# Sample-state product of the state-space phase in two f32r passes, with own room for the last group's states and tail rows

## The chip, the cores and the metric

The kernel runs on one core of a Trainium2 chip. The metric is the device time of one execution in microseconds; lower is better. The engines go by their short names: PE (TensorE, with PEld for its weight loads), DVE (VectorE), ACT (ScalarE), POOL (GpSimd), SP (SyncE, which issues most transfers; ACT issues the others).

## The reference, cut to what matters

Two layers run over a prompt of 1024 positions and 8 sample sequences of 8 positions each: a retention layer and a state-space (SSD) layer. The change is in the second. Per head, with keys `bm`, queries `cm`, values `v` and the log decay `log_a`:

```python
log_a = dt * (-jnp.exp(a_log))
v = xs * dt[..., None]
y, s_new = chunked_linear_recurrence(cm, bm, v, log_a, s0)
# inside it, per chunk (for the samples one chunk of 8 positions per sequence):
s_new = jnp.exp(cum[:, -1, :])[..., None, None] * s + jnp.einsum('bjhd,bjh,bjhe->bhde', kc, tail, vc)
```

For each of the 8 sequences the new sample state is the old one, decayed, plus keys times decayed values. The sum over the positions is the sample-state product. The outputs are y, the new states and the last three rows ahead of the convolution ("tail rows", `conv_prompt` and `conv_sample`, 27 rows of 4096 channels).

## The kernel before

The program runs in phases on one core: the first projection, the retention, its output projection (tag p2), then `phase_ssd`, then the last output projection (tag p4, `phase_mix`). Every engine has its own list of instructions, written out by hand and run in order; semaphores tie them together. `held` and `wait_ge` are waits at the head of an engine's list, so everything behind them on that engine stands too.

`phase_ssd` goes through 8 groups of 4 heads, each with 128 state rows and 4 x 64 = 256 value columns, and in each group through 8 steps c = 0 to 7, one per chunk of 128 prompt positions. In step c the samples' sequence c is done as well, so that sequences and chunks share the steps. While group g is worked on, PE also does the input projection of group g + 1 in 24 units, three per step, each of 24 f32r matmuls (`unit`, L1578); the last group (7) has none, and loads the weights of the output projection instead (`weights.load` on SP, 16 loads of 512 KB; `weights.high` on ACT and `weights.low` on DVE split them).

The samples of a group have their own chain, in step 0. PE turns keys and values (`turn`), ACT copies them to `btoks` (64 positions x 128) and `xtoks` (`by_tokens`), POOL makes the decayed values `vts` (`decayed_values`), DVE makes the sample mask, ACT its exponentials (`decay`), and DVE the decayed scores (`decay_scores`). For sequence c, ACT's `own` (L1878) multiplies the keys with a 0/1 column of that sequence into `bm`, and PE's `sample` (L1612 and L1615) makes four products of 8 columns with the old state `s_in` and then the sample-state product of `bm` (stationary) and `vts` (moving, 256 columns) in f32, over 128 rows of which the lower 64 are zero. DVE's `sample_state` adds the decayed old state (POOL's `s_mid`), and ACT stores the result. `sample(g, 0)` stands in step 1, ahead of that step's first unit; the other sequences c stand at the end of step c.

The states are loaded by SP into two slots (`load_state`, L1464); in each step the load for c + 2 waits until the slot is used, and in group 7 it stands behind three weight loads. In group 7 PE also turns 512 columns of the tail rows per step into PSUM (L1679), ACT copies them to `tail_rows` (27 x 512, L1885) and stores them with two transfers (`conv_rows_out`); the next copy waits for the stores before, and PE's next turn for the copy. At the end of the phase ACT waits for its stores. Behind step 7 DVE scales the first tile of the output projection (`next_tile.scale_all`, L2566), when ACT has made its roots (`next_tile.roots`), and the output projection begins with L2731.

Of the kernel before, what the change touches and what calls it, by code (L numbers as in the profile page):

```python
# [5 lines left out]
F32 = mybir.dt.float32  # L6
# [4 lines left out]
P = 128  # L11
# [1274 lines left out]
def phase_ssd(nc, sb, ps, sem, A, O, block0, xn_dram, params, rows_dram, dtail, lnb, etot, etot_s, g_dram, ss_dram, weights, next_tile, stale):  # L1286
# [11 lines left out]
    with ExitStack() as ctx:  # L1298
        SL = 4
        DH = 2  # L1300
        hi, lo, raw, whi, wlo, mid, th = block0.shared
        zb = block0.zb
        sb(ctx, "room_zb1", [P, NT6, CINW], F32)
        tails = sb(ctx, "p3tails", [P, CT, CTAIL], F32)
        tail_rows = sb(ctx, "p3tail_rows", [CTAIL, BANK], F32)

# [4 lines left out]
        seqcol = sb(ctx, "s_seqcol", [NS, DB], F32)  # L1311
# [20 lines left out]
        bm = sb(ctx, "s_bm", [P, 2, P], F32)  # L1332
        vt, vts = sb(ctx, "s_vt", [P, 2, SHG, SHD], F32), sb(ctx, "s_vts", [P, SHG, SHD], F32)
# [26 lines left out]
                 "sb_add", "b_own",  # L1360
# [6 lines left out]
        early, consts, passed, zeroed = sem("s_early"), sem("s_consts"), sem("s_passed"), sem("s_zeroed")  # L1367
        tails_turned, tails_taken, tails_stored = sem("s_tails_turned"), sem("s_tails_taken"), sem("s_tails_stored")
# [58 lines left out]
        def freed(eng, G):  # L1427

            if not isinstance(G, int) or G >= 2:
                held(eng, q["gated"], 9 * (G - 1) + B, passed)  # L1430

# [4 lines left out]
        with nc.Block() as block:  # L1436
            @block.sync
            def _(sp):
# [38 lines left out]
                def group(g, first=False, more=True, beyond=True):  # L1477
                    for c in range(NCH):
# [27 lines left out]
                        if c + 2 < NCH or more:  # L1506
                            load_state(g + (c + 2) // NCH, (c + 2) % NCH, 8 * g + c + 1)
# [22 lines left out]
                for dst, name in ((least_s, "least_s"), (seqcol, "seqcol")):  # L1530
                    sp.dma_start(dst[:], A[name]).then_inc(consts, 16)
# [30 lines left out]
            def _(pe):  # L1562
# [40 lines left out]
                def sample(g, c, par):  # L1603

                    s = c % 2
                    held(pe, q[f"sin{s}"], 16 * (4 * g + c // 2 + 1) + B, passed)
# [4 lines left out]
                    for k in range(NX):  # L1611
                        nc.tensor.matmul(xs_ps[:, k, c * OWN:(c + 1) * OWN], s_in[:, s, 2 * k:2 * k + 2, :].rearrange(  # L1612
                            "p h n -> p (h n)"), zb[par][:, 1, own], start=True, stop=True)
# [10 lines left out]
                def group(g, par, first=False, more=True):  # L1624
                    for c in range(NCH):
# [8 lines left out]
                        if c == 1:  # L1634
                            held(pe, q["vt"], prep(g, NCH) + 1 + B, passed)
                            sample(g, 0, par)
                        if more:
                            unit(g + 1, 3 * c)

# [30 lines left out]
                        else:  # L1670
                            sample(g, c, par)
                        if not more:
# [3 lines left out]
                            if c:  # L1676
                                pe.wait_ge(tails_taken, c)
                            for k in range(BLK):
                                last = nc.tensor.transpose(pr_ps[0:CTAIL, 0, k * P:(k + 1) * P], tails[:, c * BLK + k, :],  # L1679
# [69 lines left out]
                pe.wait_ge(zeroed, 8)  # L1749
# [11 lines left out]
            def _(act):  # L1761
# [58 lines left out]
                def by_tokens(g, c):  # L1820
# [10 lines left out]
                    nc.scalar.activation(b_dst[0:r, :], t_ps[0:r, 0:P], ACT.Copy).then_inc(q["tok"], 1)  # L1831
# [43 lines left out]
                def own(g, c):  # L1875

                    act.wait_ge(q["sb_mm"], 8 * g + c - 1 + B)
                    nc.scalar.activation(bm[0:NS, c % 2, :], btoks[:, :], ACT.Copy,  # L1878
                                         scale=seqcol[:, c:c + 1]).then_inc(q["b_own"], 1)

                def conv_rows_out(c):
                    act.wait_ge(tails_turned, c + 1)
                    if c:
                        dma_wait(act, tails_stored, 2 * c)
                    nc.scalar.activation(tail_rows[:, :], pr_ps[0:CTAIL, 0, :], ACT.Copy).then_inc(tails_taken, 1)  # L1885
                    act.wait_ge(tails_taken, c + 1)
                    at = slice(c * BANK, (c + 1) * BANK)
                    act.dma_start(O["conv_prompt"][0, 0, :, at], tail_rows[0:TAP - 1, :]).then_inc(tails_stored, 16)
                    act.dma_start(O["conv_sample"][0, :, :, at].rearrange("b w c -> (b w) c"),
                                  tail_rows[TAP - 1:CTAIL, :]).then_inc(tails_stored, 16)  # L1890

                def group(g, par, first=False, more=True, beyond=True):
                    for c in range(NCH):
# [125 lines left out]
                act.wait_ge(zeroed, 8)  # L2019
# [17 lines left out]
                dma_wait(act, tails_stored, 2 * NCH)  # L2037

            @block.gpsimd
            def _(pool):  # L2040
# [53 lines left out]
                def group(g, par, first=False, more=True):  # L2094
                    for c in range(NCH):
# [21 lines left out]
                        held(pool, q[f"sin{c % 2}"], 16 * (4 * g + c // 2 + 1) + B, passed)  # L2117
                        held(pool, q["sb_add"], 8 * g + c + B, passed)
                        nc.gpsimd.tensor_tensor(s_mid[:, :, :], s_in[:, c % 2, :, :],
# [20 lines left out]
                nc.gpsimd.memset(bm[NS:P, :, :], 0.0).then_inc(zeroed, 1)  # L2140
                nc.gpsimd.memset(vts[NS:P, :, :], 0.0).then_inc(zeroed, 1)
# [860 lines left out]
```

## Time and profile before

| | us |
|---|---|
| median of 3 runs (lowest, highest) | 2138.38 (2137.99, 2140.6) |
| profiled execution, its own time | 2143.32 |
| its span | 2141.5 |
| PE busy / DVE / ACT / POOL | 2042.8 / 1299.1 / 891.1 / 386.8 |
| mean granted PE clock | 0.976 |

The groups 0 to 6 of `phase_ssd` lie between about 1172 and 1873 us of the span, group 7 between 1873 and 1941, and the last output projection behind that. A row of a timeline has its start in us from the start of the span, its length, the engine, the line, the operation, output and inputs by name, their shapes and a count; in brackets stands the idle time ahead of it with what ended it. An f32 matmul shows as two instructions. The length of a matmul includes time in the pipeline, so the time that one holds PE is read from start to start. The profiled execution is one execution, slower than the median of the runs by 4.9.

### The profile page before, as it was taken

The numbers are of one execution on the slowest core, as the hardware profiler recorded it, in microseconds if no ns is written. First come the engines' busy times: TensorE is split into PE (matmuls) and PEld (weight loads), VectorE is DVE, ScalarE is ACT, GpSimd is POOL, SyncE is SP. The second block draws the span as 40 slices with busy tenths as digits, with TensorE's granted clock in tenths as the row PEclk, the third lists the DMA queues.
The fourth block names the chain that finished last, engine by engine and source line by source line (L and its number), as shares of the span: only waits on it lengthen the run. The fifth ranks groups of instructions, "written<-read, shape, count | busy, mean of one in ns | idle before, by whom it ended". The sixth has DMA issues, their size and how long they took to land. (4 is left out here: it accounts for less than half of the span.)

```text
span 2141.5 us, 40784 instructions
## 1 busy us (share of the span) xinstructions
PE 2042.8 (95%) x14070; PEld 1887.9 (88%) x14070; DVE 1299.1 (61%) x1929; ACT 891.1 (42%) x1947; POOL 386.8 (18%) x558
## 2 busy tenths in 40 slices
PE   6999999999899998999889999999999999978998
PEld 6999999999778776788789999999999999966887
DVE  7755899776456567233244757685767676675422
ACT  6221212333344355233344555554555555466331
POOL 0200000000122221000001434342434333350000
PEclk9999999999999998999999999999999999988999
DMA  4433333332688798243622333333333333284341
GB/s 134 132 103 103 91 101 108 107 112 82 206 278 275 248 314 296 88 143 110 176 49 62 93 85 85 84 87 85 94 93 80 96 80 88 69 263 137 115 126 40
DMA packets 387153, 274.10 MB, mean 128 GB/s; under 512 B 117714, under 2 KB 342706, under 8 KB 386922
## 3 DMA queue, kind: packets, MB, share of 16 engines
q1 hardware_dynamic: 338806, 242.77, 38.4%
q10 hardware_dynamic: 48144, 28.76, 4.4%
q8 instruction: 112, 1.84, 0.4%
q14 instruction: 91, 0.74, 0.1%
HBM read 184.59 MB, written 86.88 MB: 127 GB/s over the span
## 5 line engine op out<-in xcount | busy, mean ns | idle before, releaser
L1578 PE MATMUL p3acc_ps<-xn2hi,p3whi 128*128 128x272 f32 x1536 | 461.2, 300 | 6.2 <-ACT p3mid L1780 3.7
L1578 PE MATMUL p3acc_ps<-xn2lo,p3whi 128*128 128x272 f32 x1536 | 445.5, 290 | 0.0
L1578 PE MATMUL p3acc_ps<-xn2hi,p3wlo 128*128 128x272 f32 x1536 | 445.4, 290 | 0.0
L269 PE MATMUL p1ps<-x1hi,w1hi 128*128 128x272 f32 x1288 | 373.3, 290 | 4.7 <-issue 3.1
L269 PE MATMUL p1ps<-x1hi,w1lo 128*128 128x272 f32 x1288 | 373.1, 290 | 0.0
L269 PE MATMUL p1ps<-x1lo,w1hi 128*128 128x272 f32 x1288 | 372.1, 289 | 0.0
L1578 PEld LDWEIGHTS p3acc_ps<-xn2hi,p3whi 128*128 128x128 f32 x1536 | 292.3, 190 | 7.6 <-issue 7.2
L1578 PEld LDWEIGHTS p3acc_ps<-xn2lo,p3whi 128*128 128x128 f32 x1536 | 292.6, 191 | 0.2
L1578 PEld LDWEIGHTS p3acc_ps<-xn2hi,p3wlo 128*128 128x128 f32 x1536 | 291.8, 190 | 0.0
L269 PEld LDWEIGHTS p1ps<-x1hi,w1hi 128*128 128x128 f32 x1288 | 243.6, 189 | 5.1 <-issue 5.1
L269 PEld LDWEIGHTS p1ps<-x1hi,w1lo 128*128 128x128 f32 x1288 | 244.0, 189 | 0.0
L269 PEld LDWEIGHTS p1ps<-x1lo,w1hi 128*128 128x128 f32 x1288 | 243.6, 189 | 0.0
L2174 DVE SCALAR_TENSOR_TENSOR p3zb<-p3mid,params,p3zb 128x1112 f32<-128x1112 f32 x96 | 139.1, 1449 | 32.3 <-ACT p3zb L1792 18.8
L2064 POOL TENSOR_TENSOR s_gn<-s_yd,p3zb 128x256 f32<-128x256 f32 (+1 forms) x72 | 66.7, 926 | 316.0 <-DVE s_yd L2247 296.3
L419 ACT ACTIVATE y1sums<-p1ps 128x544 f32<-128x544 f32 x23 | 14.4, 625 | 262.2 <-PE p1ps L269 256.0
L1780 ACT ACTIVATE p3mid<-p3acc_ps 128x272 f32<-128x272 f32 x96 | 38.1, 397 | 135.6 <-PE p3acc_ps L1578 135.3
L1184 POOL MEMSET r_vlo<- 64x512 f32 x1 | 0.5, 519 | 480.9 <-POOLq L195 480.9
L2870 DVE TENSOR_TENSOR p4h<-p4h,p4acc 128x1024 f32<-128x1024 f32 (+1 forms) x9 | 11.0, 1220 | 119.1 <-PE p4acc L2731 104.3
L2731 PE MATMUL p2acc<-w2hi,p2ghi 128*128 128x512 f32 x256 | 80.7, 397 | 2.5 <-DVE p2glo L2845 2.5
L2731 PE MATMUL p4acc<-w4hi,p4ghi 128*128 128x512 f32 x256 | 80.0, 394 | 2.8 <-DVE p4glo L2845 2.8
L2731 PE MATMUL p2acc<-w2lo,p2ghi 128*128 128x512 f32 x256 | 79.8, 394 | 0.0
L2731 PE MATMUL p2acc<-w2hi,p2glo 128*128 128x512 f32 x256 | 79.5, 392 | 0.0
(330 smaller groups left out, 4367.4 us busy)
## 6 DMA issues: line engine op xcount, KB each, us to landing
w1raw<-in_ret_w_in SPq DMA_DIRECT2D x48, 512.0 KB, 5.0
p3raw<-in_ssm_w_in SPq DMA_DIRECT2D x48, 512.0 KB, 4.4
ret_vg<-y1out SPq DMA_DIRECT2D x32, 512.0 KB, 3.2
r_vg<-ret_vg SPq DMA_DIRECT2D x32, 512.0 KB, 5.0
r_sin<-in_state_ret SPq DMA_DIRECT2D x32, 512.0 KB, 6.1
out_ret_sample<-r_sout ACTq DMA_DIRECT2D x32, 512.0 KB, 6.5
s_cr<-sums SPq DMA_DIRECT2D x64, 256.0 KB, 3.4
ret_qk<-y1out SPq DMA_DIRECT2D x16, 512.0 KB, 3.7
```

The costliest lines, as they stand in the source:

```text
L269: last = nc.tensor.matmul(bank[:, 2 * at + i, 0:HB], w[s][:, idx, k, :], x[:, idx, k, i * HB:(i + 1) * HB], start=(k == 0 and j == 0), sto ...
L419: nc.scalar.activation(s1, slot(0), ACT.Copy).then_inc(s1_done, 1)
L1184: nc.gpsimd.memset(vlo[NS:P, :].bitcast(F32), 0.0).then_inc(zeroed, 1)
L1578: last = nc.tensor.matmul(pr_ps[:, n % 2, 0:TB], wt[:, j % 2, k, :], x[:, k, b * TB:(b + 1) * TB], start=(k == 0 and i == 0), stop=(k == K ...
L1780: last = nc.scalar.activation(mid[:, j % 2, TAP - 1 + b * TB:TAP - 1 + (b + 1) * TB], src, ACT.Copy)
L2064: nc.gpsimd.tensor_tensor(gn[:, slot(c), :, 0:width(c)], yd[:, :, 0:width(c)], zb[par][:, ZS:NT6, cols(c)], ALU.mult).then_inc(q["gated"], 1)
L2174: nc.vector.scalar_tensor_tensor(zb[par][:, j, 0:PW], mid[:, j % 2, w:w + PW], params[:, bass.ds(channel(G, j), 1), w], zb[par][:, j, 0:PW ...
L2731: last = nc.tensor.matmul(acc[0:r, t % 2, cols], x[:, t % 2, k, 0:r], wt[:, k, cols], start=(k == 0 and j == 0), stop=(k == KI - 1 and j = ...
L2870: nc.vector.tensor_tensor(h[0:r, t % 2, :], h[0:r, t % 2, :], acc[0:r, t % 2, :], ALU.add).then_inc(added, 1)
```

## The change

In `sample` the f32 product becomes two f32r products into the same sums. Keys and values are split into a high half, rounded to f32r, and the rest. The first product has the high key half on rows 0 to 63 and the low one on rows 64 to 127 (masked together by `own`, over 128 rows), against the high value half on both; the second has the high keys against the low values, over 64 rows. Once per group ACT copies the keys again as `bhl` (in `by_tokens`), DVE subtracts the low keys (`sample_keys_low`, behind `outputs(g, 0)` and ahead of the sample mask), ACT copies the values twice into `vhi` (`sample_values_high`, ahead of the sample exponentials) and DVE subtracts the low values (`sample_values_low`, behind `project` of step 0). `own(g, 0)` moves behind ACT's `project` of step 0, and waits for the low keys. `sample(g, 0)` moves behind the first unit of step 1 and waits for the low values (`v_low`).

In group 7 the states 2 to 7 go to a room of their own, and SP issues their six loads in step 0 ahead of the gain and the weights, once the projection is done. The tail rows get a room of 27 x 4096 and two PSUM banks by turns; they leave in two stores at the end of step 7. The room lies where the split weights go later. Two clears on POOL drop out, as no row of `bm` and `vts` is padding any more.

```diff
@@ sync
+        if c == 0:
+            sp.wait_ge(q["p_mm"], NU * SG + B)
+            for x in range(2, NCH):
+                sp.dma_start(s_in_last[:, x - 2, :, :], A["state_ssm"][0, x, g * SHG:(g + 1) * SHG, :, :
+                                   ].rearrange("h n p -> n h p")).then_inc(last_in, 16)
             sp.wait_ge(q["fin"], NT6 * SG + B)
...
-                        if c + 2 < NCH or more:
+                        if more:
                             load_state(g + (c + 2) // NCH, (c + 2) % NCH, 8 * g + c + 1)
@@ tensor, sample
-                    nc.tensor.matmul(sb_ps[:, 0:W], bm[:, s, :], vts[:, :, :].rearrange("p h n -> p (h n)"),
-                                     start=True, stop=True).then_inc(q["sb_mm"], 1)
+                    nc.tensor.matmul(sb_ps[:, 0:W], bm[:, s, :], vhi[:, :, :].rearrange("p h n -> p (h n)"), start=True, stop=False)
+                    nc.tensor.matmul(sb_ps[:, 0:W], bm[0:NS, s, :], vlo[:, :, :].rearrange("p h n -> p (h n)"),
+                                     start=False, stop=True).then_inc(q["sb_mm"], 1)
@@ tensor, group
-                        if c == 1:
-                            held(pe, q["vt"], prep(g, NCH) + 1 + B, passed)
-                            sample(g, 0, par)
                         if more:
                             unit(g + 1, 3 * c)
+                        if c == 1:
+                            held(pe, q["v_low"], g + 1 + B, passed)
+                            sample(g, 0, par, more)
...
-                            if c:
-                                pe.wait_ge(tails_taken, c)
+                            if c >= 2:
+                                pe.wait_ge(tails_taken, c - 1)
@@ scalar, by_tokens
+                    if c == NCH:
+                        last = nc.scalar.activation(bhl[0:NS, :], t_ps[0:NS, 0:P], ACT.Copy)
+                    last.then_inc(q["tok"], 1)
@@ scalar, own and the new copies
-                    nc.scalar.activation(bm[0:NS, c % 2, :], btoks[:, :], ACT.Copy,
+                    nc.scalar.activation(bm[:, c % 2, :], bhl[:, :], ACT.Copy,
                                          scale=seqcol[:, c:c + 1]).then_inc(q["b_own"], 1)
+                def sample_values_high(g):
+                    held(act, q["vt"], prep(g, NCH) + 1 + B, passed)
+                    nc.scalar.activation(vhi[0:NS, :, :], vts[:, :, :], ACT.Copy)
+                    nc.scalar.activation(vhi[NS:P, :, :], vts[:, :, :], ACT.Copy).then_inc(q["v_high"], 1)
@@ scalar, conv_rows_out
-                    if c:
-                        dma_wait(act, tails_stored, 2 * c)
-                    nc.scalar.activation(tail_rows[:, :], pr_ps[0:CTAIL, 0, :], ACT.Copy).then_inc(tails_taken, 1)
...
+                    nc.scalar.activation(tail_rows[:, c * BANK:(c + 1) * BANK], pr_ps[0:CTAIL, c % 2, :], ACT.Copy).then_inc(tails_taken, 1)
+                    if c == NCH - 1:
+                        act.wait_ge(tails_taken, NCH)
+                        act.dma_start(O["conv_prompt"][0, 0, :, :], tail_rows[0:TAP - 1, :]).then_inc(tails_stored, 16)
+                        act.dma_start(O["conv_sample"][0, :, :, :].rearrange("b w c -> (b w) c"),
+                                      tail_rows[TAP - 1:CTAIL, :]).then_inc(tails_stored, 16)
@@ scalar, group
                         if c == 0:
                             by_tokens(g, NCH)
-                            act.wait_ge(q["tok"], prep(g, NCH) + 1 + B)
-                            own(g, 0)
                         if more:
                             project(g + 1, 3 * c + 2, 1 - par, beyond)
+                        if c == 0:
+                            held(act, q["b_low"], g + 1 + B, passed)
+                            own(g, 0)
                         square(g, c)
                         if c == 0:
+                            sample_values_high(g)
                             decay(g, NCH, decs)
@@ vector
+                def sample_keys_low(g):
+                    held(dve, q["tok"], prep(g, NCH) + 1 + B, passed)
+                    held(dve, q["b_own"], 8 * g + B, passed)
+                    nc.vector.tensor_tensor(bhl[NS:P, :], btoks[:, :], bhl[0:NS, :], ALU.subtract).then_inc(q["b_low"], 1)
+                def sample_values_low(g):
+                    held(dve, q["v_high"], g + 1 + B, passed)
+                    nc.vector.tensor_tensor(vlo[:, :, :], vts[:, :, :], vhi[0:NS, :, :], ALU.subtract).then_inc(q["v_low"], 1)
...
                         outputs(g, c, par)
                         if c == 0:
+                            sample_keys_low(g)
                             held(dve, q["ins"], 16 * (g + 1) + B, passed)
                             dve.wait_ge(q["y_mm"], 9 * g + B)
                             mask(g, NCH, crws, decs, least_s[:, :])
                             decay_scores(g, NCH, decs)
                         if c + 1 < NCH and more:
                             project(g + 1, 3 * c + 2, 1 - par, beyond)
+                        if c == 0:
+                            sample_values_low(g)
```

## Rows read from the trace of the kernel before

**Rows 1.** Busy time by stages; the first line names the columns
```profile
core 0: us, PE busy (x) PEld busy (x) DVE busy (x) ACT busy (x) POOL busy (x), PEclk, DMA share, GB/s
...
1575.00:1677.00 102.00, 102.00 (x813) 100.68 (x812) 69.92 (x115) 53.65 (x135) 39.26 (x55) 1.00 0.34 87
...
1873.00:1941.00 68.00, 44.95 (x257) 37.78 (x255) 47.94 (x99) 42.28 (x112) 29.94 (x44) 0.80 0.74 226
```

**Rows 2.** Timeline of PE, group 5: start, length, engine, line, operation, operands
```profile
1699.87 0.60 PE L1648 MATMUL s_ps<-s_vt,s_btok 128*128 128x256 f32 x2
...
1700.30 0.39 PE L1594 MATMUL s_ps<-p3zb 128*128 128x128 f32 x2
...
1707.62 0.51 PE L1612 MATMUL s_ps<-p3zb,s_sin 128*128 128x8 f32 x4
1707.98 0.68 PE L1615 MATMUL s_ps<-s_vts,s_bm 128*128 128x256 f32 x2
1708.49 0.27 PE L1586 MATMUL s_ps<-s_ident,p3zb 128*128 128x128 f32 x1
...
1710.47 0.29 PE L1578 MATMUL p3acc_ps<-xn2lo,p3whi 128*128 128x272 f32 x1
1710.60 0.29 PE L1578 MATMUL p3acc_ps<-xn2hi,p3wlo 128*128 128x272 f32 x1
```

**Rows 3.** Timeline of ACT, step 0 of group 2
```profile
1377.48 0.40 ACT L1780 ACTIVATE p3mid<-p3acc_ps 128x272 f32<-128x272 f32 x1 [1.76 <-PE p3acc_ps L1578]
...
1378.08 0.30 ACT L1837 ACTIVATE s_decs<-s_decs 64x128 f32<-64x128 f32 x1
```

**Rows 4.** Timeline of DVE, step 0 of group 2 (in brackets: idle before, releaser)
```profile
1374.97 0.28 DVE L2215 TENSOR_TENSOR s_decs<-s_crws,s_least_s 64x128 f32<-64x128 f32 x1
...
1378.89 0.41 DVE L2227 TENSOR_TENSOR s_decs<-s_decs,s_ps 64x256 f32<-64x256 f32 x1 [3.64 <-ACT s_decs L1839]
1379.23 1.21 DVE L2164 TENSOR_TENSOR p3wlo<-p3raw,p3whi 128x1024 fp32r<-128x1024 f32 x1
```

**Rows 5.** Timeline of PE, start of step 1 of group 2
```profile
1377.93 0.51 PE L1612 MATMUL s_ps<-p3zb,s_sin 128*128 128x8 f32 x4
```

**Rows 6.** Timeline of DVE, the sample mask of group 6
```profile
1780.93 0.82 DVE L2215 TENSOR_TENSOR s_decs<-s_crws,s_least_s 64x128 f32<-64x128 f32 x1
```

**Rows 7.** Timeline of ACT, group 7
```profile
1880.72 0.26 ACT L1831 ACTIVATE s_btoks<-s_ps 64x128 f32<-64x128 f32 x1
...
1887.48 1.15 ACT L2444 ACTIVATE w4hi<-w4raw,hn 128x1024 fp32r<-128x1024 f32 x1 [2.02 <-DMA w4raw<-in_ssm_w_out]
...
1927.85 0.59 ACT L1885 ACTIVATE p3tail_rows<-p3acc_ps 27x512 f32<-27x512 f32 x1 [4.25 <-DMA out_conv_sample<-p3tail_rows]
```

**Rows 8.** Timeline of PE, group 7 and the start of the output phase
```profile
1882.30 0.99 PE L1612 MATMUL s_ps<-p3zb,s_sin 128*128 128x8 f32 x4 [0.15 <-issue]
...
1941.09 1.22 PE L2731 MATMUL p4acc<-w4hi,p4ghi 128*128 128x512 f32 x2 [2.83 <-DVE p4glo L2845]
```

**Rows 9.** Timeline of DVE, group 7 and the scaling behind it
```profile
1889.16 1.16 DVE L2213 SCALAR_TENSOR_TENSOR s_dec<-s_cr,lnb,s_least 128x128 f32<-128x128 f32 x2
...
1894.92 1.16 DVE L2213 SCALAR_TENSOR_TENSOR s_dec<-s_cr,lnb,s_least 128x128 f32<-128x128 f32 x2
...
1931.44 0.69 DVE L2566 TENSOR_TENSOR p4gr<-p4gr,p4ri 128x512 f32<-128x512 f32 x1 [4.03 <-ACT p4ri L2558]
```

**Rows 10.** Timeline of SP, one state load of group 7
```profile
1885.16 0.38 SPq L1464 DMA_DIRECT2D s_sin<-in_state_ssm  x1
```

**Rows 11.** Waits of group 7: engine, tile, line, releaser, us, times, longest
```profile
PE s_ps L1612 <- DMA s_sin<-in_state_ssm: 7.2, 4, 3.1
...
PE p3acc_ps L1679 <- ACT p3tail_rows L1885: 4.5, 4, 2.0
```

**Rows 12.** DMA issues: engine, count, KB each, median us to landing
```profile
out_ret_sample<-r_sout ACTq DMA_DIRECT2D x32, 512.0 KB, 6.5
...
out_y_prompt<-p4xn SPq DMA_DIRECT2D x8, 512.0 KB, 3.1
```

More of the change, by code:

```diff
@@ L1301, in phase_ssd @@
         hi, lo, raw, whi, wlo, mid, th = block0.shared
+        s_in_last, tail_rows = last_group
         zb = block0.zb
@@ L1331, in phase_ssd @@
         btoks, xtoks = sb(ctx, "s_btoks", [NS, P], F32), sb(ctx, "s_xtoks", [P, SHG * 3 * SHD], F32)
-        bm = sb(ctx, "s_bm", [P, 2, P], F32)
-        vt, vts = sb(ctx, "s_vt", [P, 2, SHG, SHD], F32), sb(ctx, "s_vts", [P, SHG, SHD], F32)
+        bhl, bm = sb(ctx, "s_bhl", [P, P], F32R), sb(ctx, "s_bm", [P, 2, P], F32R)
+        vt, vts = sb(ctx, "s_vt", [P, 2, SHG, SHD], F32), sb(ctx, "s_vts", [NS, SHG, SHD], F32)
+        vhi, vlo = sb(ctx, "s_vhi", [P, SHG, SHD], F32R), sb(ctx, "s_vlo", [NS, SHG, SHD], F32R)
         dec, decs = sb(ctx, "s_dec", [P, 2, SHG, P], F32), sb(ctx, "s_decs", [P, SHG, NS], F32)
@@ L1430, in freed, with state_arrived @@
                 held(eng, q["gated"], 9 * (G - 1) + B, passed)
+        def state_arrived(eng, g, c, more):
+            if more or c < 2:
+                held(eng, q[f"sin{c % 2}"], 16 * (4 * g + c // 2 + 1) + B, passed)
+                return s_in[:, c % 2, :, :]
+            dma_wait(eng, last_in, NCH - 2)
+            return s_in_last[:, c - 2, :, :]
         def sample_cols(s):
@@ L1601, in squares, with sample @@
                     nc.tensor.matmul(ss_ps[:, 0:r], ones[:, :], sq[:, 0, 0:r], start=True, stop=True).then_inc(q["ss_mm"], 1)
-                def sample(g, c, par):
+                def sample(g, c, par, more):
                     s = c % 2
-                    held(pe, q[f"sin{s}"], 16 * (4 * g + c // 2 + 1) + B, passed)
+                    state = state_arrived(pe, g, c, more)
                     held(pe, q["sb_add"], 8 * g + c + B, passed)
@@ L1670, in group @@
                         else:
-                            sample(g, c, par)
+                            sample(g, c, par, more)
                         if not more:
@@ L1830, in by_tokens @@
                     nc.scalar.activation(spread(x_dst[0:r, :]), t_ps[0:r, P:P + W].rearrange("p (h n) -> p h n", h=SHG), ACT.Copy)
-                    nc.scalar.activation(b_dst[0:r, :], t_ps[0:r, 0:P], ACT.Copy).then_inc(q["tok"], 1)
+                    last = nc.scalar.activation(b_dst[0:r, :], t_ps[0:r, 0:P], ACT.Copy)
+                    if c == NCH:
+                        last = nc.scalar.activation(bhl[0:NS, :], t_ps[0:NS, 0:P], ACT.Copy)
+                    last.then_inc(q["tok"], 1)
                 def decay(g, c, dst):
@@ L2116, in group @@
                             decayed_values(g, NCH)
-                        held(pool, q[f"sin{c % 2}"], 16 * (4 * g + c // 2 + 1) + B, passed)
+                        state = state_arrived(pool, g, c, more)
                         held(pool, q["sb_add"], 8 * g + c + B, passed)
-                        nc.gpsimd.tensor_tensor(s_mid[:, :, :], s_in[:, c % 2, :, :],
+                        nc.gpsimd.tensor_tensor(s_mid[:, :, :], state,
                                                 etot_s[:, c, bass.ds(g * SHG, SHG)].unsqueeze(2).to_broadcast(
@@ L2971, in program @@
             with ExitStack() as c:
+                sb(c, "room_rows", [P, (KI - LATE4) * D], F32)
+                last_group = (sb(c, "s_sin_last", [P, NCH - 2, SHG, SHD], F32), sb(c, "p3tail_rows", [CTAIL, CONVDIM], F32))
+            with ExitStack() as c:
                 whi = sb(c, "w4hi", [P, KI, D], F32R)
@@ L2980, in program @@
                     sb(c1, "room_rest", [P, 2 * KD * T + 6 * KD * P + 3 * CINW + zw - 2 * KI * D], F32)
-                    phase_ssd(nc, sb, ps, sem, A, O, block0, xn_dram, params, rows_dram, *steps, g2_dram, ss2_dram, weights, next_tile, before)
+                    phase_ssd(nc, sb, ps, sem, A, O, block0, xn_dram, last_group, params, rows_dram, *steps, g2_dram, ss2_dram, weights, next_tile, before)
                 release(before)
```

33 lines of the change are left out of this document (13 added, 20 removed).

## Prediction

> **What bounds the kernel now.** I read the busy time by stages first, then the timeline of TensorE (PE) inside one stage, then the waits of the last stage. In the table of stages, a group of the state-space phase that still projects for the next one (the row 1575 to 1677) has PE busy for its whole 102 us at a granted clock of 1.00, VectorE (DVE) for 70 and ScalarE (ACT) for 54 [rows 1]. The reader should see that there an instruction taken off PE shortens the group by its own length, and that work on DVE or ACT costs nothing until PE has to wait for it. Groups 0 to 6 are of this kind. The last one, group 7, has nothing to project: 68 us, PE busy 45, granted clock 0.80, DMA share 0.74 [rows 1]. It is a chain over ACT, DVE and the loads. So the change has two prices, one for each kind of stage, and the second isn't found by counting PE instructions.
>
> **The product itself, groups 0 to 6.** The sample-state product is one f32 matmul of 128x256, which shows as two instructions. After four small products (L1612) it holds PE from 1707.98 to 1708.49, 0.51 us; the same shape behind a long product (L1648) holds it 0.43 (1699.87 to 1700.30) [rows 2]. The 0.08 more I read as the load of the stationary tile, which eight columns don't hide. The new pair is f32r. Its nearest row is the projection, f32r and 272 columns, with a pitch of 0.13 (1710.47 to 1710.60) [rows 2]; for 256 columns that is 0.12. The pair then holds PE 0.08 + 2 x 0.12 = 0.32 and saves 0.19. If no load shows the saving is 0.27, if both loads show it is 0.11; I take 0.19, since a 0.12 us product is long enough to hide a load of 0.08. Groups 0 to 6 have 7 x 8 = 56 such products: **-10.6 us** (-6.2 to -15.1).
>
> **The new wait in groups 0 to 6.** The halves have to be made, and PE's first sample product of a group now waits for the last of them, v_low. I follow that chain through step c = 0 of group 2. ACT evacuates a unit at 1377.48 and, one squaring later, starts the sample exponentials at 1378.08: 0.30 per instruction [rows 3]. The change puts three instructions ahead of the exponentials (own, moved behind the unit, and two copies for vhi): 3 x 0.30 = 0.9. DVE's decay_scores for the samples, which waits for the exponentials, goes from 1378.89 to 1379.79. Behind it, 0.34 later, DVE makes the low weights in 1.21 (rows 1378.89 and 1379.23) [rows 4]; values_low then starts at 1381.34 and takes 0.41, as the 64x256 operation of 1378.89 does: 1381.75. PE could start step 1's sample product at 1377.93 [rows 5]; now it does a unit first, 24 x 0.125 + 0.1 = 3.1, and is there at 1381.03. It waits 0.7, and everything behind it in PE's order waits too, the next two units among them: 7 x 0.7 = **+4.9 us**. The bounds are 0.3 (faster copies) and 1.2 (below) a group: +2.1 to +8.4.
>
> What else the halves add in these groups lies under cover. The third copy by ACT (bhl) and keys_low on DVE come while PE runs unit 2; DVE waits for the copy, and behind it the sample mask is queued, but between that mask and decay_scores DVE was idle 3.64 us [rows 4]. If that cover were gone, the 0.3 us of keys_low would add to v_low's wait. Making bm for 128 rows rather than 64 costs nothing, for time goes with the columns. Dropping two clears on GpSimd comes long before they are used. Nothing for all three, with 0.3 a group already inside the bound.
>
> One rule speaks against the change. The sample mask of 64x128 took 0.28 us where it began ahead of GpSimd's product and 0.82 where it began behind it [rows 4, 6]. The Trainium skill, SBUF — State Buffer, section Who interferes with whom, says that a VectorE instruction with two SBUF inputs contends with a GpSimd instruction that reads SBUF; both new subtractions are such. By that rule a collision adds about 0.5 us to a group's wait and the sum becomes 3.8 us worse, if it falls so in every group. The two rows agree with it, but whether the subtractions meet GpSimd's work no run here shows.
>
> **The last group, start.** In group 7 the wait is longer, because the chain has no unit to run beside. The copies of the samples end at 1880.98 (1880.72 + 0.26) [rows 7]. Then follow the bhl copy (0.26, as that row), keys_low (0.28, as the mask row of that size), the mask, now behind both (0.82 beside GpSimd and an estimated 0.5 for its two small parts), the exponentials (0.7 estimated from 0.30 per instruction), decay_scores and values_low (0.41 each): 1884.4. Today the first sample product of this group starts at 1882.30 [rows 8], so it comes 2.0 later or a little more; the shorter pair gives back 0.4 at the low clock. So step 2 on DVE starts 1.6 late, against 1889.16 [rows 9]. The loads add to that. SP now issues six state loads of 0.38 us each [rows 10] ahead of the gain and the weights: the first weights go out 2.4 later (6 x 0.38 and the wait), and 768 KB go ahead of them, up to 2.6 more at some 300 KB per us, a third above the stage's mean of 226 GB/s [rows 1]. Today ACT waits 2.02 for these weights until 1887.48 [rows 7]; then it will wait 2.4 to 5.0 longer, with its decay for step 3 behind that, and behind the decay DVE's step. Without the tail stores ACT wins back about 0.8. Either way DVE is d = 1.6 to 4.2 late after step 2.
>
> **The last group, later steps.** Removed are PE's waits for states (7.2 us in four) and for the tail copy (4.5) [rows 11], and ACT's for the tail store (4.25) [rows 7]. They don't simply add up, since DVE's own step of 5.76 (1889.16 to 1894.92, without a gap) [rows 9] is next: that is where a stall that goes leaves the end. The steps 2 to 6 take 5 x 5.76, step 7 an estimated 4.4, since it makes no mask (1.16 for two heads alone), so DVE could start scaling the next phase's tile at 1889.16 + 28.8 + 4.4 + d = 1924.0 to 1926.6. It started at 1931.44, 4.03 of it waiting for ACT [rows 9], whose roots stood behind the wait that ended at 1927.85 [rows 7]. The gain there is 4.8 to 7.4, middle 6.1. The tail rows now leave in two stores of 432 KB in all (27 rows of 4096), and ACT waits for them at the end of the phase. The trace has no landing for such a store; the nearest rows, stores of 512 KB, have 3.1 and 6.5 [rows 12]. Issued 3.9 after the start of the scaling, they let the first product of the output phase come 8.9 to 12.3 after it, today 9.65 (1931.44 to 1941.09) [rows 8, 9]: 0 to 2.7 of loss, I take 0.9, near the shorter row, as the queue is emptier then. In all **-5.2 us** (-2.1 to -7.4). Everything behind PE's start at 1941.09 moves with it.
>
> **The sum.** -10.6 + 4.9 - 5.2 = **-10.9 us** on the profiled execution, whose own time is 2143.3 (span 2141.5): 2132.4. The median of the runs shown is 2138.4, 4.9 lower, and I put the same difference under it: 2127.5, so I predict **2127.5 us**.
>
> **The rivals.**
> 1. The loads take the last group's gain. For it speaks that the DMA share is already 0.74 in that stage and that ACT waits for the first weights today [rows 1, 7]; against it that only the first weights meet the new loads. If ACT's step 2 is 7 us late rather than 1.6 to 4.2, the 5.2 is gone: -5.7, 2132.7.
> 2. v_low comes in time and the loads of the stationary tile hide. The gain is then 56 x 0.27 = 15.1 and the wait 0.3 a group: -15.1 + 2.1 - 5.2 = -18.2, 2120. For it: the projection shows no load at all. Against: L1615 shows 0.08 today [rows 2], and two copies can't shrink much below 0.2.
> 3. The pair is no shorter, that is the change doesn't do what it says on PE, say because changing from f32 to f32r and back costs what the passes save. Then +4.9 - 5.2 = -0.3, 2138. Against it: the projection follows f32 products all along at its usual pitch.
> 4. Slower: the wait for v_low takes the place of the passes removed. Its place is PE's sample(g, 0) in step 1, where the whole of PE's order stands. It eats the gain of a group from 8 x 0.19 = 1.5 us on, and the whole gain from (10.6 + 5.2) / 7 = 2.3 us on. At 3.2 a group, 2.5 more than worked out, the sum is -10.6 + 22.4 - 5.2 = +6.6, 2145. That would need ACT's copies or DVE's chain to be a further 2.5 late, as when both copies wait for GpSimd's vts and every DVE operation meets GpSimd. The slack rows, DVE idle 3.64 ahead of decay_scores [rows 4], speak against.
>
> **How the numbers follow.** A collision of both subtractions with GpSimd alone (0.5 a group as between the two mask rows, -10.9 + 3.8 = -7.1, 2131) lies in the forecast's spread, with 0.1 of its chance. The forecast has 0.62, rival 1 0.14, rival 2 0.12, rival 3 0.06, rival 4 0.06. A measurement of this kernel can tell about 0.2%, 4.3 us, from no change. The forecast's own spread, with -9.5 to -12.3 for the pair, +3.5 to +7 for the wait and -2.1 to -7.4 in the last group, is -4.6 to -16.2, or 2122 to 2133.7, faster throughout; rival 1 is faster in most of its span, rival 3 no change. The range from 2117 to 2134 takes in rivals 1 and 2 and leaves out rivals 3 and 4. Faster 0.85, same 0.09, slower 0.06.
>
> **What would show it.** Right: in groups 0 to 6, the two product instructions over 0.3 us instead of 0.51; one PE wait a group on DVE's s_vlo of about 0.7 us and no other; the group some 0.8 us shorter. In group 7: no wait on s_sin from step 2 on, none on the tail copy, DVE at 5.8 us a step without gaps, one ACT wait on the first weights of 4 us or more. Wrong: a v_low wait of over 1.5 us; a product pair near 0.5; ACT waiting for weights again in step 2; a wait for the tail stores of over 3 us at the end of the phase.

## The result, and the profile after

The change makes the kernel slower. Its median is 2171.24 us (2169.21 to 2177.23, four runs), that of the kernel before in the same comparison 2139.49; the ratio is 1.0155, with an interval from 1.0134 to 1.0175. The prediction was 2127.5 with a range to 2134, so the sign is wrong. The profiled execution of the change took 2169.21 us (span 2167.4, mean granted clock 0.973).

I divide a trace by PE's first turn of the samples of each group (L1586 before, L1599 after, the only turn into 64 columns). From there to the next is a group; group 7 ends with the first product of the output phase. A second trace was taken of each kernel (both are among the experiments). The third group holds a PE stall of 1.6 to 2.2 us that waits for nothing the profile shows, in every trace, and the seventh projects less; the first row of the table is of the other five.

| us | before | the change |
|---|---|---|
| one group, of the five | 101.03, in both traces | 103.8 to 105.6 |
| groups 0 to 6 together | 707.9 and 710.0 | 737.8 and 737.9 |
| group 7 | 61.4 and 63.8 | 61.7 and 60.6 |

So groups 0 to 6 lose 29 us, where -5.7 was forecast, and group 7 gains about 1.5 on the means, less than its two traces of before differ by, where -5.2 was forecast. Ahead of group 0 little is changed (the two clears on POOL drop out there), and that stretch is 1162 to 1176 us long in the traces of this study, without order.

The table of stages of the change, one group and the stage of group 7, answers [rows 1]:

```profile
core 0: us, PE busy (x) PEld busy (x) DVE busy (x) ACT busy (x) POOL busy (x), PEclk, DMA share, GB/s
1695.34:1800.81 105.47, 104.15 (x805) 101.13 (x805) 70.50 (x116) 53.22 (x135) 38.24 (x54) 0.98 0.32 84
1898.70:1966.70 68.00, 42.68 (x255) 35.49 (x253) 48.27 (x100) 42.37 (x114) 31.08 (x44) 0.78 0.76 223
```

PE is still the bound of the group, but it now idles 1.3 us in it, and its granted clock is 0.98 instead of 1.00. Those are two of three causes. The third is in the product, on PE and on the weight loads (PEld), against [rows 2]; the length of a matmul is read from start to start:

```profile
1714.91 0.51 PE L1625 MATMUL s_ps<-p3zb,s_sin 128*128 128x8 f32 x4
1715.28 0.37 PE L1628 MATMUL s_ps<-s_vhi,s_bm 128*128 128x256 f32 x1
1715.57 0.38 PE L1629 MATMUL s_ps<-s_vlo,s_bm 64*128 64x256 f32 x1
1715.88 0.33 PE L1599 MATMUL s_ps<-s_ident,p3zb 128*128 128x128 f32 x1
...
1715.25 0.19 PEld L1628 LDWEIGHTS s_ps<-s_vhi,s_bm 128*128 128x128 f32 x1
1715.57 0.18 PEld L1629 LDWEIGHTS s_ps<-s_vlo,s_bm 64*128 64x128 f32 x1
1715.88 0.14 PEld L1599 LDWEIGHTS s_ps<-s_ident,p3zb 128*128 128x128 f32 x1
```

The pair holds PE from 1715.28 to 1715.88, 0.60 us, and the f32 product it replaces held it 0.51. In the projection a load begins about 0.1 ahead of its product, while the one before still runs. Here the load of the 64-row operand begins with its product, at 1715.57, and so does the next load of 128 rows, at 1715.88: neither is covered by the product before it.

PE's start of step 1, group 5, answers [rows 5]:

```profile
1702.29 0.28 PE L1591 MATMUL p3acc_ps<-xn2hi,p3wlo 128*128 128x272 f32 x1
1703.90 0.58 PE L1625 MATMUL s_ps<-p3zb,s_sin 128*128 128x8 f32 x4 [1.32 <-DVE s_vlo L2277]
1704.34 0.36 PE L1628 MATMUL s_ps<-s_vhi,s_bm 128*128 128x256 f32 x1
...
1704.94 1.19 PE L1658 MATMUL s_ps<-p3zb,s_S 128*128 128x128 f32 x4
...
1707.44 0.43 PE L1591 MATMUL p3acc_ps<-xn2lo,p3whi 128*128 128x272 f32 x1
1707.67 0.43 PE L1591 MATMUL p3acc_ps<-xn2hi,p3wlo 128*128 128x272 f32 x1
```

PE waits 1.32 for the low values. Behind the wait the pitch of the projection is 0.23 (1707.44 to 1707.67) instead of 0.13 [rows 2], until 1708.35. The granted clock in 4.5 us behind the wait, four of the seven groups:

```profile
1175.81:1180.31 4.50, 4.50 (x32) 4.19 (x33) 3.04 (x7) 2.52 (x6) 0.91 (x4) 1.00 0.45 110
1279.73:1284.23 4.50, 4.50 (x24) 4.19 (x25) 2.74 (x5) 2.73 (x6) 1.80 (x4) 0.72 0.36 88
...
1494.36:1498.86 4.50, 4.50 (x32) 4.19 (x33) 2.77 (x5) 2.73 (x6) 1.83 (x4) 1.00 0.34 83
1598.47:1602.97 4.50, 4.50 (x20) 3.97 (x21) 1.59 (x4) 2.63 (x6) 0.65 (x2) 0.62 0.31 70
```

In five of seven groups (means of 0.62 to 0.75) half of the stretch or more runs at the lower of the clock's two levels, 1.2 instead of 2.4 GHz; two stay at 1.00. The groups at 1.00 are those of 103.8 and 104.0 us, the slower ones those of 105.5 to 105.6.

### The profile page after: what moved, and what is told of

Read it like the earlier page. It is cut to its first block and busy times, and to the rows that moved or that the text cites. A ratio compares the mean times of both kernels' runs of the same rounds, so it can differ in the third digit from the quotient of the medians.

```text
span 2167.4 us, 40832 instructions
## 1 busy us (share of the span) xinstructions
PE 2056.6 (95%) x14070; PEld 1890.7 (87%) x14070; DVE 1300.4 (60%) x1945; ACT 896.7 (41%) x1971; POOL 389.5 (18%) x556
## 5 line engine op out<-in xcount | busy, mean ns | idle before, releaser
L2763 PE MATMUL p4acc<-w4lo,p4ghi 128*128 128x512 f32 x256 | 79.8, 393 | 0.0
```

The costliest lines, as they stand in the source:

```text
L2763: last = nc.tensor.matmul(acc[0:r, t % 2, cols], x[:, t % 2, k, 0:r], wt[:, k, cols], start=(k == 0 and j == 0), stop=(k == KI - 1 and j = ...
```

## The experiments

Theory A: the 64-row operand makes the pair long. Theory B: the wait for the low values, and the lower clock as its consequence, is the rest. Theory C: the last group's part eats its own gain. Each ran beside the kernel before, whose median was 2142.88 (27 runs) beside the second product over 128 rows, the low values earlier, both, and the last group's part; 2143.96 (7) beside the product twice, the kernel before again, the weights first, and the stores on SP; and 2141.58 (7) beside the other four.

**The second product over 128 rows.**

```diff
-        vhi, vlo = sb(ctx, "s_vhi", [P, SHG, SHD], F32R), sb(ctx, "s_vlo", [NS, SHG, SHD], F32R)
+        vhi, vlo = sb(ctx, "s_vhi", [P, SHG, SHD], F32R), sb(ctx, "s_vlo", [P, SHG, SHD], F32R)
...
-                    nc.tensor.matmul(sb_ps[:, 0:W], bm[0:NS, s, :], vlo[:, :, :].rearrange("p h n -> p (h n)"),
+                    nc.tensor.matmul(sb_ps[:, 0:W], bm[:, s, :], vlo[:, :, :].rearrange("p h n -> p (h n)"),
...
+                nc.gpsimd.memset(vlo[NS:P, :, :].bitcast(F32), 0.0).then_inc(zeroed, 1)
```

> The change, with the second product over 128 rows: the low values get 64 rows of zeros below them (cleared once), and the stationary operand is all of bm. Theory A (the 64-row stationary operand makes its own load and the next one show, so that the pair holds PE 0.60 us): the pair falls to about 0.32 (0.24 to 0.40), the transposes behind it by 0.05 a step; 56 x 0.28 to 0.33 = 16 to 18 us less than the change, 2171 - 17 = 2154. The wait for the low values stays at 1.3 to 1.5 a group, with the lower clock behind it. Rival (the loads show because an f32r product follows f32 ones or adds into the same sums, whatever the rows): the pair stays at 0.60 and the time at 2171.

2142.02 us, ratio 0.9995 (0.9976 to 1.0013): 34 below the change by the ratios (give or take 6), not 17. PE in a step:

```profile
1694.26 0.37 PE L1628 MATMUL s_ps<-s_vhi,s_bm 128*128 128x256 f32 x1
1694.46 0.29 PE L1629 MATMUL s_ps<-s_vlo,s_bm 128*128 128x256 f32 x1
1694.59 0.27 PE L1599 MATMUL s_ps<-s_ident,p3zb 128*128 128x128 f32 x1
```

The pair holds 0.20 + 0.13 = 0.33, and theory A stands: twice the rows are faster. The waits are as before (1.32 to 1.47), yet most groups take 101.0 to 101.2. Groups 0 to 6 take 711.3 together, 26.5 less than in the change. Of these 20 are the row count's (0.36 for each of 56, below). The rest goes with the clock: behind the same wait it now falls in two groups of seven (0.68 and 0.66) and not in five. Why it does so less often isn't shown.

**The low values earlier on DVE.**

```diff
                             mask(g, NCH, crws, decs, least_s[:, :])
+                            sample_values_low(g)
                             decay_scores(g, NCH, decs)
                         if c + 1 < NCH and more:
                             project(g + 1, 3 * c + 2, 1 - par, beyond)
-                        if c == 0:
-                            sample_values_low(g)
```

> The change, with DVE's subtraction of the low values moved ahead of the decayed sample scores (and so ahead of the low weights). Its input is there at 1700.72 of the trace of the change, so it ends near 1701.1, and PE comes to it at 1702.6. Theory B (the lower granted clock of 3 to 4 us in most groups is the consequence of PE's idle 1.3 us): the wait of 1.3 to 1.5 a group goes (10.0 us in seven groups) and the time at the lower clock with it (about 10 us), and group 7 waits 1 less: 2171 - 20 = 2151, granted clock 1.00 throughout groups 0 to 6. Rival (the clock falls for another reason, such as the loads that show): only the wait goes, 2161, with stretches at the lower clock left. The pair stays at 0.60.

2146.86 us, ratio 1.0026 (1.0007 to 1.0044), 28 below the change. No wait for the low values is left in groups 0 to 6, groups take 102.3, and the granted clock is 1.00 over the ten us around step 1 in all seven. So wait and clock go together, as theory B says; they cost 737.8 - 718.3 = 19.5 us in the seven groups, against 4.9 in the sum.

The stall of the third group says the same without the wait. PE idles in it for 1.6 to 2.2 us in every kernel, and the granted clock was lower in the 4.5 us behind it in 11 of the 14 traces (means of 0.62 to 0.70), with the f32 product, with the 64-row pair and with both passes over 128 rows. In the second trace of the kernel before:

```profile
1468.38 0.30 PE L1586 MATMUL s_ps<-s_ident,p3zb 128*128 128x128 f32 x1 [2.05 <-issue]
...
1468.38:1472.88 4.50, 4.50 (x23) 4.30 (x24) 1.37 (x4) 0.55 (x2) 0.92 (x2) 0.62 0.33 67
```

So a fall needs neither the pair nor the wait. The length of the idle time doesn't decide alone either: the clock stayed at 1.00 behind 1.64 us in the first trace of before, 1.78 with the second product over 128 rows, and 2.03 in the last group's part alone.

**Both.** The two diffs above together.

> Both edits on the change: second product over 128 rows, and the low values ahead of the decayed sample scores. If theories A and B hold and their savings add: 2171 - 17 - 20 = 2134, faster than the kernel before (2139) by what the pair saves in groups 0 to 6, 56 x 0.19 = 10.6, less what group 7 loses (PE is over its full clock only in part of it) and less any rest of the wait. If rival A holds (pair stays at 0.60) 2151; if rival B holds 2144.

2125.81 us, ratio 0.9928 (0.9908 to 0.9948): faster than before, and 8 below the 2134 expected. Groups take 99.44, which is 1.59 less than before, and 0.20 for each of eight products. Against the run before it (102.30) the row count alone costs 2.86 a group, 0.36 a step: 0.28 in the pair, the rest in what follows. Groups 0 to 6 take 698.3 together.

**The 64-row product twice**, in the kernel with the low values early.

```diff
+                    nc.tensor.matmul(sb_ps[:, 0:W], bm[0:NS, s, :], vlo[:, :, :].rearrange("p h n -> p (h n)"), start=False, stop=False)
                     nc.tensor.matmul(sb_ps[:, 0:W], bm[0:NS, s, :], vlo[:, :, :].rearrange("p h n -> p (h n)"),
                                      start=False, stop=True).then_inc(q["sb_mm"], 1)
```

> The change with the low values made early, and the 64-row product issued twice in a row (so the low part of the samples' states is added twice: the output is off in the last bits only). Groups take 102.3 us without the doubling. If every 64-row stationary operand shows its load, the third product holds PE 0.31 like the second: +2.5 a group, 104.8. If only a change of the row count shows (128 to 64 and 64 to 128), the third costs its 256 columns, 0.11 to 0.12: +0.9 to 1.0 a group, 103.3.

```profile
1707.00 0.37 PE L1628 MATMUL s_ps<-s_vhi,s_bm 128*128 128x256 f32 x1
1707.29 0.38 PE L1629 MATMUL s_ps<-s_vlo,s_bm 64*128 64x256 f32 x1
1707.52 0.28 PE L1630 MATMUL s_ps<-s_vlo,s_bm 64*128 64x256 f32 x1
1707.72 0.33 PE L1599 MATMUL s_ps<-s_ident,p3zb 128*128 128x128 f32 x1
...
1707.29 0.18 PEld L1629 LDWEIGHTS s_ps<-s_vlo,s_bm 64*128 64x128 f32 x1
1707.40 0.19 PEld L1630 LDWEIGHTS s_ps<-s_vlo,s_bm 64*128 64x128 f32 x1
1707.72 0.14 PEld L1599 LDWEIGHTS s_ps<-s_ident,p3zb 128*128 128x128 f32 x1
```

2160.27 us in one run. Groups take 103.23, 0.93 more, 0.12 a step: the third product costs its columns. The second 64-row load begins 0.11 behind the first and is covered; the loads that show are those where the row count changes, from 128 to 64 and back.

**The change again**, for a second trace.

> The change itself, for a second trace. If the lower clock behind the wait for the low values is a property of the change, it comes again in most of groups 0 to 6 (5 of 7 in the first trace), with 1.3 to 1.5 us of idle PE ahead of it each time, and the groups take 103.8 to 105.6 us; if it was chance, in few or none and the groups take 103.8.

2172.83 us in one run. Groups of 103.8 to 105.6; behind the waits of 1.32 to 1.53 the clock fell in five groups again (0.63 to 0.74), not quite in the same ones.

**The kernel before again.**

> The kernel before, unchanged, for a second trace. In its first trace group 0 began at 1171.8, in the five traces since at 1162 to 1168, though nothing is changed ahead of it. If that part varies from execution to execution (its granted clock in the retention was 0.95 in one trace and 1.00 in others), this trace begins group 0 anywhere from 1162 to 1172 and its groups take 101.0 us again; if the layout of the kernel before is behind it, 1171 to 1172 again.

2148.20 us in one run. Group 0 began at 1171.4, groups took 101.03. With later traces at up to 1175.6, the stretch ahead varies by execution. Group 7 took 63.8 and not 61.4, so single traces of group 7 differ by 2.4 for the kernel before.

**The last group's part alone**, on the kernel before: the hunks of the diff on the six loads, on `conv_rows_out` and on the tail rows' turns, and no others.

> The kernel before with the last group's part alone: own room for states 2 to 7 and for the tail rows, six state loads ahead of the gain and the weights, two tail stores at the end; the product stays f32, without halves. Theory C (the first weights come 3.4 us later behind the six state loads, DVE's later steps take 6.1 instead of 5.76, and ACT's transfer issues at the end take 2 longer, so that the gain is eaten inside this part): 2137 to 2140, no difference from before. Rival (the part gains its 5.2 us, and only the longer chain of the halves in group 7 took it): 2134, with the output phase's first product 5 us nearer to the group's start than the 61.4 of before.

2136.93 us, ratio 0.9976 (0.9958 to 0.9995): a gain, of 1 to 9 us by the interval, and the trace has 0.9 to 3.3 of it in group 7 (60.5). What stands against it, in ACT's timeline:

```profile
1883.06 1.15 ACT L2454 ACTIVATE w4hi<-w4raw,hn 128x1024 fp32r<-128x1024 f32 x1 [6.52 <-DMA w4raw<-in_ssm_w_out]
```

ACT waits 6.5 for the first weights, behind six state loads, against 2.0 [rows 7]. The two answers aren't told apart by the time.

**The tail rows' room alone.** Both edits, with the states in their slots.

```diff
-                        if more:
+                        if c + 2 < NCH or more:
                             load_state(g + (c + 2) // NCH, (c + 2) % NCH, 8 * g + c + 1)
...
-                    state = state_arrived(pe, g, c, more)
+                    held(pe, q[f"sin{s}"], 16 * (4 * g + c // 2 + 1) + B, passed)
```

> Both edits on the change, with the states of group 7 in their two slots again, loaded as before; only the tail rows keep their own room. If the room for the states is worth something, PE waits for states again (7 to 8 us in the traces of before) and group 7 takes 60 to 62 us from its first turn to the output phase, against 58.7 with both rooms. If the tail rows alone give what the last group gained, 58 to 59.5.

2129.47 us in one run. PE's waits in group 7:

```profile
PE s_ps L1621 <- DMA s_sin<-in_state_ssm: 10.4, 5, 5.2
```

Group 7 takes 63.7 against 58.7, more than either answer expected, so the states' room is worth 5.0 between these two traces (the two of the kernel before differ by 2.4). The tail rows' room alone shows no gain against the 61.4 and 63.8 of before.

**The weights first.** Both edits, and SP's six state loads behind the first three weight loads.

```diff
                             for k in range(3 * c, min(3 * c + 3, KI)):
                                 weights.load(sp, k)
+                            if c == 0:
+                                sp.wait_ge(q["p_mm"], NU * SG + B)
+                                for x in range(2, NCH):
...
```

> Both edits of the run before on the change, and in group 7 SP's six state loads behind the gain and the first three weights rather than ahead of them. In the trace with both edits ACT waited 3.8 us for the first weights, in the last group's part alone 6.5, in the kernel before 2.0. Theory C (those loads make the first weights late, and all later steps with them): the wait falls to 2 or less and group 7, from its first turn to the first product of the output phase, goes from 58.7 to 55 to 57 us; 2125.8 - 2.5 = 2123. Rival (the longer chain of the halves sets step 2, or the states now come late): group 7 stays within 0.5 us of 58.7, or PE waits for states.

2125.42 us, ratio 0.9907 (0.9875 to 0.9939); group 7 took 59.1. ACT's wait fell to 1.0, but PE now waits 1.1 for states, and DVE begins step 3 at 18.0 us of the group instead of 17.6. The rival holds: the order of the loads alone gives nothing.

**The tail stores on SP.** As that, and:

```diff
                 group(7, more=False)
+                sp.wait_ge(tails_taken, NCH)
+                sp.dma_start(O["conv_prompt"][0, 0, :, :], tail_rows[0:TAP - 1, :]).then_inc(tails_stored, 16)
...
```

> As the run with the weights first, and the two tail stores issued by SP behind its last step instead of by ACT ahead of its last square. With ACT the four transfers in a row took 3.3 us to issue and the square waited 3.7 for them; in the kernel before it waited 1.8. Theory: the square comes 1.9 earlier and the output phase with it: another 1 to 1.9 us off group 7, 2121. Rival (the product of the output phase waits for SP's own loads, which now stand behind the tail stores, or for their landing): nothing or up to 1 us later.

2125.09 us, ratio 0.9910 (0.9880 to 0.9939); group 7 took 58.6. The last square comes 1.6 earlier, but the first product then waits 4.4 for its operand instead of 3.3: 0.5 is left of it. The phase's end waited for something else.

**The tail rows stored in three parts.**

```diff
+                def store_tails(a, b):
+                    sp.wait_ge(tails_taken, b)
+                    at = slice(a * BANK, b * BANK)
...
+                            if c in (4, 7):
+                                store_tails(c - 4, c - 1)
...
+                store_tails(6, 8)
```

> As the run with SP's stores, with the tail rows stored in three parts: 1536 columns in step 4, 1536 in step 7, 1024 at the end, instead of 4096 at the end. From the scaling to the first product of the output phase it took 9.65 us before, 11.9 to 12.0 in every kernel with the two whole stores, 11.6 with SP's. Theory: the last state store lands 4.3 to 5.1 us after its issue, instead of 2.1, because 432 KB of tail rows go beside it, and ACT's wait for it holds the output phase: with 108 KB at the end it takes 9.7 to 10.5, group 7 56.5 to 57.5, time 2123.5. Rival (the phase's end waits for something else): 11.6 again.

```profile
1907.88 3.42 DVE L2604 TENSOR_TENSOR p4gr<-p4gr,p4ri 128x512 f32<-128x512 f32 x4 [0.28 <-DMA p4gr<-g2T]
...
1917.34 1.22 PE L2769 MATMUL p4acc<-w4hi,p4ghi 128*128 128x512 f32 x2 [2.54 <-DVE p4glo L2883]
```

From the scaling to the first product 9.46, group 7 56.8: the theory stands: it was the whole tail stores that held the end of the phase. 2123.71 us, ratio 0.9920 (0.9890 to 0.9949).

**The states two by two.**

```diff
-                            if c == 0:
-                                sp.wait_ge(q["p_mm"], NU * SG + B)
-                                for x in range(2, NCH):
+                            if c < 3:
+                                if c == 0:
+                                    sp.wait_ge(q["p_mm"], NU * SG + B)
+                                for x in range(2 * c + 2, 2 * c + 4):
```

> As the run with the tails spread, and the six states of group 7 loaded two each in steps 0, 1 and 2, behind the weights of the step, each pair with its own count. With all six at once, ahead of the weights or behind them, DVE began step 3 at 17.6 to 18.4 us of the group, before at 15.3 and 15.6. Theory: whichever of the two goes second holds steps 2 and 3 (768 KB of states), so with a third of them in step 0 step 3 begins 1 to 2 earlier and the phase ends as much earlier: another 1 to 2 off, 2122. Rival (the chain of the halves and the product's wait for the low values hold step 3): 17.6 again and no change.

2122.43 us, ratio 0.9897 (0.9870 to 0.9923), the lowest median. DVE begins step 3 at 16.6, 1.3 earlier than in the run before, as the theory said; 0.8 of it is left at the scaling and 0.5 at the end of group 7 (56.3). Where the other 0.8 goes wasn't followed. By their times the timed kernels with both edits aren't told apart.

## Why the prediction was wrong

**The product.** I said -10.6: 0.32 for the pair instead of 0.51. The pair took 0.60, and with the wait away groups were 1.27 longer than before, +8.9 in seven. The step that failed is the price of the second pass, taken from a projection whose operands all have 128 rows; its bounds, too, held only the load of 0.08 that the f32 product shows. Two loads (0.18 and 0.14 in the rows above) show, because the row count changes twice in each step, and no row that I used had such a change in it. With 128 rows in both passes 0.33 and -1.59 a group (-11.1) were measured: the arithmetic was right for another kernel. The Trainium skill, TensorEngine Tiling (Array Packing), section Tiling Modes, says that a change of the tiling mode drains TensorE. A 64-row operand between 128-row ones fits that rule if it counts as such a change, which no trace names; the loads agree with it, at 0.36 a step for the way there and back. I hadn't weighed it.

**The wait.** I said 0.7 a group; it was 1.3 to 1.5. The chain was the right one, and two terms were small. ACT and DVE in step 0 of group 5 (the wait above):

```profile
1698.99 0.40 ACT L1794 ACTIVATE p3mid<-p3acc_ps 128x272 f32<-128x272 f32 x1 [2.18 <-PE p3acc_ps L1591]
...
1699.89 0.40 ACT L1900 ACTIVATE s_vhi<-s_vts 64x256 fp32r<-64x256 f32 x1
1700.30 0.42 ACT L1901 ACTIVATE s_vhi<-s_vts 64x256 fp32r<-64x256 f32 x1
1700.74 0.31 ACT L1854 ACTIVATE s_decs<-s_decs 64x128 f32<-64x128 f32 x1
...
1701.90 1.21 DVE L2184 TENSOR_TENSOR p3wlo<-p3raw,p3whi 128x1024 fp32r<-128x1024 f32 x1
1703.03 0.41 DVE L2277 TENSOR_TENSOR s_vlo<-s_vts,s_vhi 64x256 fp32r<-64x256 f32 x1
```

The two copies hold ACT 0.41 and 0.44, not 0.30, so the low values end 4.45 behind the evacuation (1703.44) and not 4.27. From there to PE's product at 1703.90 another 0.46 passes, for which the sum had nothing. The copies were done at 1700.72; DVE's low weights, 1.13 from start to start, stood ahead of the subtraction though nothing asks for that. The collision with GpSimd that I weighed isn't in it: the subtraction takes 0.41.

**The clock.** The sum had no term for it. It was lower behind the wait in five groups of seven, twice, and in step 1 of no group without the wait. Wait and clock cost 19.5, not 4.9; some 10 of it is the wait, the rest the clock.

**Rival 4** named that wait and its place and gave 3.2 a group as its price. With the clock it cost 2.8. **Rival 3**, the pair no shorter, came too, and worse. Each had 0.06 and a sum of its own, and their case together had none: 8.9 + 19.5 - 1.5 = +26.9. The traces give 28.9 - 1.5 = +27.4, the ratio +29 to +37. What lies between isn't in the last output projection (200.4 and 201.2 us before, 200.7 and 201.0 after) and isn't located.

**The last group.** The delay d in step 2 was within its bounds: 13.48 us behind the first turn against 9.50, so 4.0, and ACT's wait on the weights is there (2.87, later by 3.4). Three terms behind it were too small. I show DVE's steps, ACT's issues at the end and PE:

```profile
1918.49 1.16 DVE L2233 SCALAR_TENSOR_TENSOR s_dec<-s_cr,lnb,s_least 128x128 f32<-128x128 f32 x2
...
1920.98 1.66 DVE L2482 SCALAR_TENSOR_TENSOR w4lo<-w4raw,hn,w4hi 128x1024 fp32r<-128x1024 f32 x1
...
1924.60 1.16 DVE L2233 SCALAR_TENSOR_TENSOR s_dec<-s_cr,lnb,s_least 128x128 f32<-128x128 f32 x2
...
1954.65 1.54 DVE L2598 TENSOR_TENSOR p4gr<-p4gr,p4ri 128x512 f32<-128x512 f32 x2 [1.17 <-ACT p4ri L2590]
...
1960.31 1.52 ACTq L1962 DMA_DIRECT2D out_ssm_prompt<-s_S  x1
...
1966.68 1.22 PE L2763 MATMUL p4acc<-w4hi,p4ghi 128*128 128x512 f32 x2 [3.31 <-DVE p4glo L2877]
```

A step takes 6.11 (1918.49 to 1924.60) and not 5.76, since the low weights take 1.66 and not 1.28 in three of six steps, and in another DVE waits 0.34 for PE. The kernel before has such long ones in two of its six steps, so the step that I priced from [rows 9] was a light one:

```profile
1912.09 1.62 DVE L2450 SCALAR_TENSOR_TENSOR w4lo<-w4raw,hn,w4hi 128x1024 fp32r<-128x1024 f32 x1
```

Beside the low weights of the change, GpSimd:

```profile
1920.95 0.61 POOL L2077 TENSOR_TENSOR s_vt<-s_xtok,dtail 128x256 f32<-128x256 f32 x1 [0.23 <-DVE s_S L2304]
1921.52 1.60 POOL L2129 TENSOR_TENSOR s_Sdec<-s_S,etot 128x256 f32<-128x256 f32 x1
```

The product that began just ahead of the low weights took its usual 0.61, they took 0.38 longer, and the next product, behind their start, 1.60. The Trainium skill, SBUF — State Buffer, section Who interferes with whom, calls the port that DVE and GpSimd share an exclusive lock, and these rows agree.

Ahead of the scaling DVE waited 1.17 for ACT's roots (0.31 in the second trace), for which the sum had nothing. And from the scaling to the first product it took 12.03, not the 9.65 before plus my 0.9: the stores of 432 KB at the end were the term sized from rows of another place. With them in three parts it was 9.46. With d at 4.0 the sum left a gain of 4.2; five steps of 0.35, the 1.17 and 1.5 at the end take 4.4 of it away. What was right: the tail stores' wait was worth removing (step 6 to the scaling took 11.7, before 15.8, and 10.8 with the tail rows' room alone), and so were the waits for states (63.7 against 58.7 above). In the last kernel, with its loads and stores spread, group 7 takes 56.3 against 61.4 and 63.8, so the forecast gain was there to be had.

**Two slips in the sums.** The 8.9 and 12.3 behind the scaling hold 1.9 us beyond the 3.9 and the landing, and no row is given for them. And by the same sum rival 1's 7 us of lateness leave 1.2 of the 5.2; it takes 8.2 to eat it all. Neither moves the result.

## What to carry to other kernels

A product on half the rows isn't half a price: between products of 128 rows it shows its load and the next one's, and zeros in the other half were 0.28 us a pair cheaper. A wait added on the engine that bounds the stage is costed to the start of its next instruction, with what the clock does behind it, and its inputs go ahead of whatever else their engine has in line. A transfer collected at the end of a phase must be priced where it lands, not where it is issued.

## What the runs showed of the hardware that was not expected

The row count's change was the first (0.36 us a step). The second is the clock: PE idle for 1.3 to 1.5 us and then back to work had its granted clock at the lower level in five groups of seven with the 64-row pair behind the wait, in two of seven with the shorter pair, although idle and work were otherwise the same. What decides between two such groups wasn't settled; the stall of 1.6 to 2.2 us in the third group had it too, in 11 traces of 14, with every form of the product. The third is a transfer's issue: ACT's last store of 128 KB took 1.52 us to issue behind the whole tail stores on its queue, 1.17 with those on SP's, and 0.45 with the tail rows spread, as before the change (0.68 in the last kernel).
